# Letting the first four projections of a two-block fp32 kernel take turns

## What is computed

```
h = rms_norm(x, norm1_g)                  # x: 256 x 1024
z = h @ w_in                              # w_in: 1024 x 7168
a = a_val * sigmoid(a_gate)               # the first 2048 columns of z
a = causal_depthwise_conv(a, conv_w, conv_b)   # 31 taps for each of 1024 channels
...                                       # q, k, v, attention, output, FFN, second block
```

## Time and profile before

| | us |
|---|---|
| median of 3 runs | 829.71 (829.58 to 833.06) |
| profiled execution, its own time | 830.8 |
| its span | 829.0 |
| PE busy | 818.0 (99%) |
| DVE busy | 649.4 (78%) |
| ACT busy | 554.0 (67%) |

### The profile page before, as it was taken

One profiled execution on the slowest core, in us unless ns is written; L12 is line 12 of the kernel. 1 busy time (PEld: TensorE's weight loads), 2 busy tenths in 40 slices (PEclk: granted clock), 3 DMA queues, 4 the chain that ended last, 5 costly groups with the idle time before them and its releaser, 6 DMA issues.

```text
span 829.0 us, 16592 instructions
## 1 busy us (share of the span) xinstructions
PE 818.0 (99%) x6010; PEld 764.2 (92%) x6010; DVE 649.4 (78%) x1172; ACT 554.0 (67%) x1022; POOL 228.6 (28%) x245
## 2 busy tenths in 40 slices
PE   8999999999999999999999999999999999999996
PEld 8998998999999999999889989999998988888886
DVE  7998989997979998787766978756689866666552
ACT  8777999996756776666555776386647665655442
POOL 0387852332312244333101000020022333322110
PEclk9999999999999999999999999999999999999999
DMA  7666654546565376555646445435446566665741
GB/s 271 218 197 194 179 172 141 160 141 197 155 200 185 129 224 201 186 181 176 229 159 222 153 157 176 132 124 179 127 144 193 178 209 193 182 199 165 234 135 51
DMA packets 43168, 146.12 MB, mean 176 GB/s; under 512 B 4928, under 2 KB 7632, under 8 KB 43088
## 3 DMA queue, kind: packets, MB, share of 16 engines
q1 hardware_dynamic: 42192, 144.13, 55.0%
q10 hardware_dynamic: 896, 0.94, 0.4%
HBM read 144.00 MB, written 1.05 MB: 175 GB/s over the span
## 4 chain that ended last, share of the span: by engine, by line
PE 89%; DVE 5%; ACT 4%; issue 2%; DMA 1%; SPq 0%; DVEq 0%; ACTq 0%
PE px L561 20%; PE px L565 17%; PE px L567 16%; PE px L566 16%; PE px L562 10%; DVE wlo L1466 2%; PE px L571 1%; PE px L573 1%; PE px L572 1%; PE px L638 1%; PE px L787 1%; ACT whi L941 1%; DVE hx L1734 1%; PE px L650 1%; DMA raw<-ws 1%
## 5 line engine op out<-in xcount | busy, mean ns | idle before, releaser
L1466 DVE TENSOR_TENSOR wlo<-raw,whi 128x1024 fp32r<-128x1024 f32 x265 | 331.2, 1256 | 26.7 <-ACT whi L941 26.6
L941 ACT ACTIVATE whi<-raw 128x1024 fp32r<-128x1024 f32 x265 | 278.1, 1052 | 53.6 <-PE px L562 25.8
L565 PE MATMUL px<-hx,whi 128*128 128x256 f32 x1024 | 293.7, 287 | 0.9 <-DVE hx L1483 0.3
L566 PE MATMUL px<-hx,whi 128*128 128x256 f32 x1024 | 286.5, 280 | 0.0
L567 PE MATMUL px<-hx,wlo 128*128 128x256 f32 x1024 | 285.7, 279 | 0.0
L565 PEld LDWEIGHTS px<-hx,whi 128*128 128x128 f32 x1024 | 192.6, 188 | 4.5 <-issue 1.6
L566 PEld LDWEIGHTS px<-hx,whi 128*128 128x128 f32 x1024 | 192.9, 188 | 0.5
L567 PEld LDWEIGHTS px<-hx,wlo 128*128 128x128 f32 x1024 | 192.8, 188 | 0.0
L2119 POOL TENSOR_TENSOR CA<-CA,ct 128x256 f32<-128x256 f32 x90 | 89.9, 999 | 97.5 <-DVE wlo L1466 72.5
L561 PE MATMUL px<-fx,whi 128*128 128x512 f32 x330 | 114.5, 391 | 0.0
L561 PE MATMUL px<-hx,whi 128*128 128x512 f32 x320 | 111.1, 391 | 0.0
(11 more groups left out here) (331 smaller groups left out, 1319.1 us busy)
## 6 DMA issues: line engine op xcount, KB each, us to landing
raw<-ws SPq DMA_DIRECT2D x265, 512.0 KB, 3.6
tb<-tabs SPq DMA_DIRECT2D x16, 128.0 KB, 3.5
X<-xs SPq DMA_DIRECT2D x4, 256.0 KB, 4.0
raw<-ws SPq DMA_DIRECT2D x3, 256.0 KB, 5.7
out<-Y SPq DMA_DIRECT2D x1, 384.0 KB, 2.4
vc<-vecs SPq DMA_DIRECT2D x1, 315.5 KB, 7.0
raw<-ws ACTq DMA_DIRECT2D x1, 256.0 KB, 4.1
msk<-lmask ACTq DMA_DIRECT2D x1, 256.0 KB, 2.9
```

The source lines that it names most:

```text
L565: e.matmul(b[:, 0:S], H, xh, start=first, stop=False)
L566: e.matmul(b[:, 0:S], H, xl, start=False, stop=False)
L941: e.activation(whi[:, n % NSL, :], raw[:, n % NRAW, :], ACT.Copy).then_inc(s_hi, 1)
L1466: e.tensor_tensor(wlo[:, n % NSL, :], raw[:, n % NRAW, :], whi[:, n % NSL, :], ALU.subtract).then_inc(s_lo, 1)
```

## The change

- `HALVED` goes from 2 to 4: chunks 0 to 3 come in halves, and the first half of chunk 0 is split in two quarters. `PIECES` lists these nine pieces, `PIECES_AT` says behind which input tile ACT and DVE work on them.
- `FOUR` = ag0, av0, ag1, av1 take turns: two input tiles of each, then the next two. `spot` lays their blocks out so: chunk 0 holds k = 0 and 1 of all four jobs, chunk 3 holds k = 6 and 7. The host lays out the weights so, and `milestones` follows that order.
- SP's queue alternates input tiles and weight halves; the half that ACT issued goes to SP.
- `sums("n1")` comes after all four jobs.
- `EARLY` goes from 3 to 4: eight jobs run without 1 / rms.
- `WARM` goes from 16 to 8.
- ACT's squares of x move in between the pieces.
- The list of ACT and DVE after 1 / rms is written anew.
- `conv_plan`: taps begin at chunk 8, where they began at chunk 6; the quotas are higher.

```diff
-HALVED = 2
-WARM = 16
-EARLY = 3
+HALVED = 4
+PIECES = [(0, 0, 256), (0, 256, 512), (0, 512, CW)] + [(c, h, h + CW // 2) for c in range(1, HALVED) for h in (0, CW // 2)]
+WARM = 8
+EARLY = 4
+FOUR = [("ag", 0), ("av", 0), ("ag", 1), ("av", 1)]
+PIECES_AT = {0: PIECES[0:1], 1: PIECES[1:3], 2: [], 3: PIECES[3:4], 4: PIECES[4:5], 5: PIECES[5:6], 6: PIECES[6:7],
+             7: PIECES[7:8]}
...
+def spot(key, k, kt, at, w):
+    if key in FOUR:
+        return k // 2 * CB + 2 * FOUR.index(key) + k % 2
+    return at + k * w
...
-        quota = (2.2 if c < 12 else 3.2 if c < 24 else 2.6 if c < 34 else 3.7, 2.0 if c < 34 else 1.8)
+        quota = (2.7 if c < 12 else 3.2 if c < 24 else 2.9 if c < 34 else 3.7, 2.1 if c < 24 else 2.0 if c < 34 else 1.85)
...
-            for i in range(EARLY):
-                job(("ag", i), AX, first_scaled if i == 0 else None, rings=(FEW,))
+            for k in range(0, KD, 2):
+                for key in FOUR:
+                    job(key, AX, first_scaled if key == FOUR[0] else None, rings=(FEW if key[0] == "ag" else SMALL,),
+                        tiles=(k, k + 1))
+            sums("n1", VALUES)
+            for i in range(2, EARLY):
+                job(("ag", i), AX, rings=(FEW,))
                 job(("av", i), AX, rings=(SMALL,))
-                if i == 0:
-                    sums("n1", VALUES)
...
             for i in range(3):
+                if i == 2:
+                    piece_low(*PIECES[-1])
                 e.wait_ge(s_sq, i + 2)
...
             e.wait_ge(s_rms, 1)
+            first_tiles((0, 1, 2), ())
             early(("ag", 0), sg[:, 0, :])
+            early(("ag", 1), sg[:, 1, :])
+            first_tiles((), (0, 1, 2))
+            lows(6)
+            first_tiles((3, 4, 5), ())
             early(("av", 0), CI[:, 0, 30:])
-            first_tiles((0, 1), ())
-            first_tiles((2,), (0, 1))
-            lows(4)
...
             tiles(0)
+            half_load(0, 0)
+            half_load(0, 1)
             tiles(1)
+            half_load(1, 0)
             tiles(2)
+            half_load(1, 1)
             tiles(3)
...
```

More of the change, by code:

```diff
@@ L148, in milestones @@
         where[key] = (kt, at, w)
-        for k in range(kt):
-            final[(at + k * w) // CB] = (key, k)
+    order = [(key, k, spot(key, k, *where[key]) // CB) for key, k in block_order(placed)]
+    for key, k, c in order:
+        final[c] = (key, k)
     n, ends, used, blocks = 0, {}, {}, {}
-    for key, (kt, at, w) in where.items():
-        for k in range(kt):
-            c = (at + k * w) // CB
-            if final[c] == (key, k) or k == kt - 1 or key in BEHIND:
-                n += 1
-                blocks[key, k] = n
-                if final[c] == (key, k):
-                    used[c] = n
-        ends[key] = n
+    for key, k, c in order:
+        end = k == where[key][0] - 1
+        if final[c] == (key, k) or end or key in BEHIND:
+            n += 1
+            blocks[key, k] = n
+            if final[c] == (key, k):
+                used[c] = n
+            if end:
+                ends[key] = n
     return where, ends, used, blocks
@@ L539, in take, with job @@
                 return px[b]
-            def job(key, xs, ready=None, rings=None):
+            def job(key, xs, ready=None, rings=None, tiles=None):
                 kt, at_, w = WHERE[key]
                 rings = rings or (JOBS, JOBS)
-                banks = [take((key, t), rings[t]) for t in range(1 if w == 1 else 2)]
-                for k in range(kt):
+                tiles = tiles or range(kt)
+                if tiles[0] == 0:
+                    banks = [take((key, t), rings[t]) for t in range(1 if w == 1 else 2)]
+                else:
+                    banks = [px_of[key, t] for t in range(1 if w == 1 else 2)]
+                for k in tiles:
                     if ready:
                         ready(k)
-                    c, o = (at_ + k * w) // CB, (at_ + k * w) % CB * P
-                    if c < HALVED and o in (0, CW // 2):
-                        e.wait_ge(s_lo, 2 * c + 1 + (o > 0))
+                    b = spot(key, k, kt, at_, w)
+                    c, o = b // CB, b % CB * P
+                    if c < HALVED:
+                        for piece in PIECES:
+                            if piece[:2] == (c, o):
+                                e.wait_ge(s_lo, PIECE[piece])
                     elif c >= HALVED and c != seen[0]:
@@ L927, in _, with piece_high @@
             made = [HALVED]
-            def half_high(n, h):
-                e.wait_ge(s_raw[n] if h else s_half[n], 16)
-                e.activation(whi[:, n, half(h)], raw[:, n, half(h)], ACT.Copy).then_inc(s_hi, 1)
+            def piece_high(n, a, b):
+                e.wait_ge(s_half[n] if a < CW // 2 else s_raw[n], 16)
+                e.activation(whi[:, n, a:b], raw[:, n, a:b], ACT.Copy).then_inc(s_hi, 1)
             def highs(c):
@@ L1452, in _, with piece_low @@
             made = [HALVED]
[L1454 to L1456 removed]
+            def piece_low(n, a, b):
+                e.wait_ge(s_hi, PIECE[n, a, b])
+                e.tensor_tensor(wlo[:, n, a:b], raw[:, n, a:b], whi[:, n, a:b], ALU.subtract).then_inc(s_lo, 1)
             def lows(c):
@@ L1558, in _ @@
             e.tensor_scalar(qg8[:, :], vec("qg"), -0.125, None, ALU.mult).then_inc(s_cst, 1)
-            early(("av", 2), CI[:, 2, 30:])
-            early_gated(2)
+            e.wait_ge(s_ci, 1)
+            early(("ag", 3), sg[:, 0, :])
+            lows(9)
+            early(("av", 3), CI[:, 3, 30:])
+            early_gated(3)
             def taps(c):
@@ L2303 @@
     ws = np.zeros((n_chunks, P, CW), np.float32)
-    for _, name, cols, kt, at in placed:
+    for key, name, cols, kt, at in placed:
         w = a[name][0]
```

93 lines of the change are left out of this document (46 added, 47 removed).

## The result

The changed kernel takes 832.87 us (median of 12 runs, 832.03 to 833.64) where the kernel before, in the same set of runs, takes 829.64 (12 runs). The ratio is 1.0036, 95% interval 1.0028 to 1.0044: 3.0 us slower, by the interval 2.3 to 3.7 (the two medians lie 3.2 us apart). That is still within half a per cent, but it is no "no change", and it is above the range of the prediction. A second set of runs (e12) gave 1.0043 [1.0030, 1.0055]. The profiled execution's own time is 833.64 us, its span 831.8; of before 830.8 and 829.0.

What follows compares the result with a forecast made beforehand. PE, busy 99% of the span, was taken as the bound. The opening's 1.85 us gain was given back at chunk 9 (34.6 against 34.55), + 0.05 us, nothing elsewhere: median 829.71 became 829.8 us, range 828.0 to 831.5.

Steps and rivals of the forecast that it cites:

- The pace and the opening: Start of PE's work: 2.83 us a chunk, first real matmul at 5.2, chunk 4 at 18.45, a 1.85 us gain.
- The list of DVE: DVE's work behind 1 / rms: 15.05 us from 19.5, chunk 9's low part ends at 34.55, gain given back whole.
- the hole of 0.53 us: DVE's idle time ahead of the third `early_gated`, counted in the list; absent or twice would be 0.5 us either way.
- The signs that I had named: First matmul 5.2, chunk 3's last half around 16, `rst` 19.5, largest PE wait 2.0 us at chunk 9, starting 34.6.
- I cost it at nothing: The convolution's taps: same 155 on DVE and 93 products on ACT in 47 chunks instead of 49, taken as 0 us.
- DVE's cushion: Cover for denser taps: before, chunk 10's low part was done at 34.5, 2.9 us ahead of PE.
- taps too dense: Rival, 8%: waits of 0.3 to 0.5 us at three to five more scores and turned probabilities, 831.0 to 831.6.
- The clock: Rival, 10%: with the shorter warm-up PE's clock stays low until three pieces are done, + 1.8 us, 831.6.
- the gain stays: Rival, 15%: DVE's list 2 us shorter, no PE wait at chunk 9, 1.9 us stay, 827.8.
- bounds on the opening alone: Transfers holding ACT back or not, - 0.8 to + 0.7, and the hole, 0.5 either way: together 828.4 to 830.9.

Runs made afterwards that it cites:

- e12: The changed kernel run again, unchanged, in a second set of runs: 833.23 us, ratio 1.0043.
- e7: Changed kernel with the bank mended, chunk 9 earlier in the list, and products and additions started at chunk 6 with the old quota: 830.26 us, 1.0003.
- e10: Changed kernel with the bank mended and every second GpSimd addition of tiles 1 and 4 cut to two columns: 831.57 us, 1.0019.
- e11: Kernel before, with every second GpSimd addition of tiles 1 and 4 cut to two columns: 829.60 us, 0.9998.
- e9: Kernel before, with the bank counter set so that ao 1 and ao 2 share px1: 830.39 us, 1.0009.
- e8: e7 with 12 warm-up matmuls in place of 8: 830.29 us, 1.0001 against the kernel before.
- e4: Changed kernel with chunk 9's low part on DVE and high part on ACT one place earlier in the list: 832.44 us, 1.0035.
- e6: Kernel before with only DVE's taps as in the changed kernel, later start and higher quotas: 830.54 us, 1.0001.

## Why the prediction was wrong

- **The pace and the opening were right**, for an execution in which the clock rises early. Forecast: 5.2, 16.1, 18.45, chunk 9 at 34.6 with a wait of 2.0; the profile: 5.37, 16.36, 18.54, 34.76 with 1.7. In all five executions with that list chunk 9 comes 16.22 us behind chunk 4; my working gave 16.15. The list of DVE is the bound there and swallows the gain, as I said. Within that, `rst` came 0.45 us later than I said (19.95), and the list behind it was 0.4 us shorter, since the hole of 0.53 us ahead of the third gated tile did not recur; that the two cancel is luck. The signs that I had named came true within 0.5 us, and none of them lay behind chunk 10, where most of the loss is.
- **The step that failed: the taps, "I cost it at nothing".** I covered it with DVE's cushion, because DVE is the engine that works on low parts. I never followed the other half of the plan: products on ACT, additions on GpSimd. I looked at PE's waits and at the opening. The trace of before has it plainly: ACT waits 2.96 us for a GpSimd addition, one chunk ahead of the copies of v. An edit that starts such a chain two chunks later needed one question, whether its end can come as early relative to the chunks. 30 additions take 42.8 us, 15 chunks; with 15 chunks in place of 16 in the plan, nothing is left. In place of nothing, the plan cost 0.5 us at the score, 0.5 at the turned probability, 0.2 at chunk 57 and up to 0.6 at the head sum.
- **The number of products.** I counted 93 products in both plans and stopped. The place matters: one product more stands in the chunks ahead of a turned probability for which PE already waited, and ACT has no pause there. That is 0.5 us. My rival "taps too dense" had the place and the size of single waits right (0.3 to 0.5 us at three to five places, 831.0 to 831.6); it had 8%, and no place in it was worked out.
- **Missed altogether: the bank.** Twelve takes in place of thirteen from the ring of three. It stands in the code, not in the trace of before: 0.7 us.
- **The clock.** I set it as a case for all or nothing with 10%, and 831.6. It is part of each run instead: chunk 4 came at 18.40 to 19.75 us with eight warm-up matmuls, and as a mean this is 0.45 us later than I forecast (18.90 over the five of the account). Two of the seven profiled executions with eight warm-ups (e7, e10) showed the low clock to 10 us or beyond, the full form of the rival; its price at chunk 4 was 1.3 us in e10, where I said 1.8. The matmuls of the warm-up don't settle the point: with sixteen the pace changed near 4 us in four executions, near 5.0 in e11 and near 7.3 in e9 (seven starts or fewer in each microsecond from 4 to 7 us), where it was still warming up; with twelve near 7.1 in e8. The longer warm-up hid most of such a late rise (e9 began chunk 4 at 20.54, before at 20.41), the shorter one lays it open. The Trainium skill ("TensorE: Matmul & The Clock Gate", the part on the HAM clock gate) says that the point of the rise differs between runs of one kernel, and these traces agree.
- **The rival "the gain stays"** would not have been at 827.8 with a faster list alone: e4 shows that, with this chain, a gain of 1 us at chunk 9 ends at the head sum.
- **The range** ended at 831.5, because it was made from bounds on the opening alone, and took an edit with no row behind it at zero to both sides. The median lies 1.4 us above it.

**What stays open.** The slack of 44.4 us is read from thirteen executions of different kernels, not from an experiment that moves the chain's end alone. The step at chunk 57 is argued from the traces: PE's last block of ao 0 needs the last low part that DVE writes to `ax`, which stands behind DVE's last tap. It is done at 196.96 in the kernel before and 197.48 in e6; in e7 it is done at 197.80, but PE comes there 0.5 us later too. No run moves it alone. Why e7's and e8's chunk 9 came 0.8 us later behind chunk 4 than e4's was not isolated either; the additions that they put beside DVE's list are the suspect, as expected before the run.

## What to carry to other kernels

When an edit moves the start of a chain that runs over several engines, add up the chain on its slowest engine in its own durations, find in ACT's and GpSimd's waits who waits for its end, and compare that place, not the total of the plan's quotas. Where buffers or banks are handed out in turn, one take more or fewer at the start shifts every later pairing; list which of them meet. And a gain in an opening counts only up to the next place that is set by something else: list those places first.
